# Leaving out the idle matrix products behind the spreading of the roots at three stage boundaries

## The reference

```python
for i in range(DEPTH):                                   # 2 layers
    h = _modulate(_rmsnorm(x, norm1_w[i]), sh1, sc1)     # the same for ctx
    y, yc = _retention(...) if i == 0 else _neighbourhood_attention(...)
    x = x + g1 * y
    h2 = _modulate(_rmsnorm(x, norm2_w[i]), sh2, sc2)
    x = x + g2 * _conv_ffn(h2, ...)
    if not last:                                         # layer 0 only
        ctx = ctx + cg1 * yc  # and its own norm and FFN
return _rmsnorm(x, final_norm_w)

def _rmsnorm(x, w):
    y = x * lax.rsqrt(jnp.mean(x * x, axis=-1, keepdims=True) + NORM_EPS)
    return y * w
```

## Time and profile before

| | |
|---|---|
| median of 3 runs | 1993.24 us (1992.49 to 1995.27) |
| the profiled execution: its own time | 1995.75 us |
| its span (first to last instruction) | 1993.8 us |
| TensorE busy | 1966.0 us, 99% of the span |
| VectorE busy | 1288.7 us, 65% |
| ScalarE busy | 718.4 us, 36% |
| idle products of `keep_busy` | 62, all by line 471 |
| mean granted TensorE clock | 0.996 of full |

### The profile page before, as it was taken

How to read it: one execution, slowest core, us unless ns; L and a number is a source line. 1 busy time by engine, 2 the same in 40 slices (tenths; PEclk the granted TensorE clock), 3 DMA queues, 4 the chain that set the end, 5 groups by cost and what they waited for, 6 DMA issues and landing times.

```text
span 1993.8 us, 29041 instructions
## 1 busy us (share of the span) xinstructions
PE 1966.0 (99%) x10628; PEld 1686.2 (85%) x10628; DVE 1288.7 (65%) x1976; ACT 718.4 (36%) x1111; POOL 93.2 (5%) x161
## 2 busy tenths in 40 slices
PE   9999999999999999999999999999999999999998
PEld 8888888888888888888888888888888778888886
DVE  7866645735645677765665467867777777467376
ACT  5433224223313343312331233365665543233243
POOL 0000000000000000000000000211111000000000
PEclk9999999999999999999999999999999999999999
DMA  7221321321221123233223323331111322223223
GB/s 310 99 85 64 106 64 54 106 73 55 85 95 64 54 64 95 95 124 115 94 94 122 116 95 127 123 99 52 53 48 48 106 85 95 95 95 103 86 95 106
DMA packets 51268, 186.56 MB, mean 94 GB/s; under 512 B 5680, under 2 KB 5680, under 8 KB 51184
## 3 DMA queue, kind: packets, MB, share of 16 engines
q1 hardware_dynamic: 37744, 136.73, 20.5%
q0 software_dynamic: 13440, 48.63, 7.5%
HBM read 181.15 MB, written 4.19 MB: 93 GB/s over the span
## 4 chain that ended last, share of the span: by engine, by line
PE 94%; DVE 2%; ACT 1%; DMA 1%; issue 1%; SPq 0%; DVEq 0%; ACTq 0%; POOLq 0%
PE acc L404 60%; PE acc L724 6%; PE o_ps L543 4%; PE acc L664 4%; PE o_ps L574 3%; PE acc L543 3%; PE o_ps L724 2%; PE acc L561 2%; PE acc L503 2%; PE acc L759 1%; PE o_ps L710 1%; PE o_ps L689 1%; PE acc L697 1%; DMA ada_start<-in_ada_first_dram 1%; PE o_ps L455 1%
## 5 line engine op out<-in xcount | busy, mean ns | idle before, releaser
L883 ACT ACTIVATE w_hi<-raw 128x1024 fp32r<-128x1024 f32 x223 | 236.0, 1058 | 582.1 <-PE acc L404 466.5
L404 PE MATMUL acc<-h_hi,w_hi 128*128 128x512 f32 x1520 | 434.3, 349 | 3.4 <-ACT u L1084 1.8
L1314 DVE TENSOR_TENSOR w_lo<-raw,w_hi 128x1024 fp32r<-128x1024 f32 x223 | 272.9, 1224 | 252.7 <-ACT w_hi L883 251.1
L404 PE MATMUL acc<-h_hi,w_lo 128*128 128x512 f32 x1520 | 434.9, 349 | 0.0
L404 PE MATMUL acc<-h_lo,w_hi 128*128 128x512 f32 x1520 | 433.5, 348 | 0.0
L404 PEld LDWEIGHTS acc<-h_hi,w_hi 128*128 128x128 f32 x1520 | 244.6, 188 | 44.0 <-ACT u L1084 2.5
L404 PEld LDWEIGHTS acc<-h_hi,w_lo 128*128 128x128 f32 x1520 | 244.1, 188 | 38.2
L404 PEld LDWEIGHTS acc<-h_lo,w_hi 128*128 128x128 f32 x1520 | 243.4, 188 | 38.5
L1486 DVE SCALAR_TENSOR_TENSOR x<-acc,mod,x 128x512 f32<-128x512 f32 (+3 forms) x137 | 82.0, 634 | 149.7 <-PE acc L404 120.8
L404 PE MATMUL acc<-act_hi,w_hi 128*128 128x512 f32 (+1 forms) x396 | 119.8, 356 | 1.3 <-DVE x L1486 1.3
L404 PE MATMUL acc<-act_hi,w_lo 128*128 128x512 f32 (+1 forms) x396 | 120.1, 357 | 0.0
(11 more groups left out here) (263 smaller groups left out, 3390.8 us busy)
## 6 DMA issues: line engine op xcount, KB each, us to landing
raw<-in_weights_dram SPq DMA_DIRECT2D x232, 512.0 KB, 3.4
ada_raw<-in_ada_dram POOLq DMA_DIRECT2D x80, 512.0 KB, 3.8
ada_start<-in_ada_first_dram SPq DMA_DIRECT2D x8, 1024.0 KB, 19.2
x<-in_x_in_dram SPq DMA_DIRECT2D x4, 768.0 KB, 7.1
park_dram<-x POOLq DMA_DIRECT2D x1, 2048.0 KB, 8.1
rel<-in_bias_dram POOLq DMA_DIRECT2D x16, 128.0 KB, 2.4
x<-park_dram POOLq DMA_DIRECT2D x2, 1024.0 KB, 6.8
out_dram<-x SPq DMA_DIRECT2D x8, 256.0 KB, 2.2
```

The source lines that it names most:

```text
L404: mm = nc.tensor.matmul(tile[:, c0:c0 + cn], wt[:, b * P:(b + 1) * P], mv[:, n, c0:c0 + cn], start=(n == 0 and m == 0), stop=(n == last an ...
L883: nc.scalar.activation(w_hi[i][:, :] if spare is None else spare[0], raw[r][:, :], ACT.Copy).then_inc(hi_split, 1)
L1314: nc.vector.tensor_tensor(lo, raw[r][:, :], hi.bitcast(F32), ALU.subtract).then_inc(lo_split, 1)
```

## The change

The idle products that stand between `spread_roots` and the next stage's first projection are left out at the three inner boundaries: 12, 12 and 8 of them. Those ahead of the spreading (4 within `final_sums`, 2 behind it) stay, as does everything on the other engines. No wait and no semaphore count changes, and the result is the same.

```diff
             final_sums(TOK)
             keep_busy(2)
             spread_roots(PARTS, True)
-            keep_busy(12)
+
             ffn(PARTS, spare1)
             final_sums(TOK)
             keep_busy(2)
             spread_roots(PARTS, True)
-            keep_busy(12)
+
             q = []
...
             final_sums(LAT)
             keep_busy(2)
             spread_roots(LATENT)
-            keep_busy(8)
+
             ffn(LATENT, spare3)
```

## The result

The changed kernel takes 1996.96 us in the median of 21 runs (1994.25 to 1998.17), the kernel before 1994.17 us in 21 runs interleaved with them (1992.49 to 1996.36). The ratio is 1.0013, 95% interval 1.0007 to 1.0019: slower by 0.13%, some 2.8 us. The 0.5 us flatters the forecast: the difference was forecast as +4.3 us and measured as +2.8, 1.5 less, and 0.9 of that is hidden because the kernel before came out at 1994.17 here and not at the 1993.24 that the forecast started from. That part is luck.

What follows compares the result with a forecast made beforehand. TensorE was taken to bound the kernel (94% of the chain). Removal gains 0; clock falls cost 1.3 + 1.5 + 1.5 = +4.3 us, added to the median 1993.24: 1997.5 us, range 1992.8 to 2000.4.

Steps and rivals of the forecast that it cites:

- The removed work was hidden: At the three inner boundaries, the 8.07 us of idle products lie beside the VectorE and ScalarE chain; removal takes nothing off.
- I take 0: Gain from an earlier first product at the three boundaries: 0 to 0.45 us possible in all, taken as 0.
- The pause brings the clock down: TensorE pauses of 3.30, 3.80 and 2.54 us at the boundaries are followed by its clock falling to 0.50.
- The likeliest case: A clock fall at each of the three boundaries, +4.3 us in all, own range +3.0 to +5.5; chance 0.46.
- The rival that nothing happens: At the boundaries the pauses are too short for the clock to fall, and 1993.2 us stays; chance 0.13.
- the spared third fall: The third boundary's 2.54 us pause brings no fall, the other two do: +2.8 us, 1996.0 us; chance 0.17.
- The pause at 7 us: From 7 to 9 us TensorE did nothing and the clock stayed 1.00, so about 2 us can be free.
- The rate: Under dense work, pairs start every 0.64 us at half clock, 0.35 at full: 0.45 us lost per us.
- The sum (+4.3): Net cost of falls at the three boundaries: 1.3, 1.5 and 1.5 us, together +4.3 us.
- the mean with a long fall: First boundary: mean of a short fall, 1.54 us, and a half-hidden long one, 2.3, less 0.6 of waiting.
- The fall at 1305 us: In the attention's first projections, half clock for 3.40 us in the profiled execution; may be absent in others.
- the pause at 1302 us: 1302.22 to 1304.75 us, 2.53 us with only transposes: one pause if transposes don't count, otherwise two under 1 us.

Runs made afterwards that it cites:

- double: 24, 24 and 16 idle products of 512 columns instead of 12, 12 and 8 in the kernel before; 1996.16 us against 1994.30, ratio 1.0009.
- plain: The kernel before with 48, 48 and 32 instructions of 128 columns in place of its idle products behind the spreadings; 1995.73 us against 1994.30, ratio 1.0005.
- fill: The kernel before plus 3 idle products each ahead of and behind the attention's first six transposes; 1993.56 us against 1994.30, ratio 0.9997.
- again: The changed kernel timed once more, without edits; 1996.81 us against 1993.46 for the kernel before, ratio 1.0016.
- b2: The kernel before without the 12 idle products of the second boundary only; 1993.62 us against 1993.85, ratio 1.0001.
- bare: The changed kernel also without the idle products ahead of the spreading, at all four boundaries; 1998.26 us against 1993.46 for the kernel before, ratio 1.0026.
- half: 6, 6 and 4 idle products instead of 12, 12 and 8 in the kernel before; 1995.45 us against 1993.46, ratio 1.0010.
- plain12: The kernel before with 24, 24 and 16 plain instructions of 128 columns in place of its idle products; 1993.70 us against 1993.85, ratio 1.0000.
- narrow: The kernel before with 24, 24 and 16 instructions of 64 columns in place of its idle products; 1994.49 us against 1993.85, ratio 1.0002.
- turned: The kernel before with 24, 24 and 16 transposes of 128 columns in place of its idle products; 1993.58 us against 1994.30, ratio 0.9999.

## Why the prediction was right, point by point

**The removed work was hidden.** Right: first products at 3.29 and 2.54 us behind the spreading as before, at the first and third boundary. `double` shows the other edge of the same fact.

**"I take 0"** for a gain. Wrong by 0.2 us at the second boundary. There the first product came 3.58 us behind the spreading instead of 3.80, and 3.57 to 3.66 in each run with none or only 6 of the 512-column products at that place and the ones ahead of the spreading kept (`plain` apart, whose filler outlasted the operand). Unlike elsewhere, VectorE reads the latent half of `x` and of the roots column by column there. Its four first multiplications (L1461), in the kernel before and in the changed one:

```profile
1274.38 3.00 DVE L1461 SCALAR_TENSOR_TENSOR scratch<-x,norm_a,o_ps 128x512 f32<-128x512 f32 x4 [1.25 <-PE o_ps L455]
```

```profile
1274.21 2.77 DVE L1461 SCALAR_TENSOR_TENSOR scratch<-x,norm_a,o_ps 128x512 f32<-128x512 f32 x4 [1.25 <-PE o_ps L455]
```

The same four took 2.99 us in `fill` and 2.93 in `double`, 2.77 to 2.78 in `again`, `b2` and `bare`, and 2.79 to 2.86 beside shorter or fewer products; at the first boundary they took 2.19 us with and without them. So the idle products slowed the chain that was to hide them, by 0.23 us; the prediction had dismissed this on the ground that VectorE begins first. What they compete for was not tried.

**The pause brings the clock down.** Right, and at all three boundaries, in two profiles. The likeliest case, a fall at each, was the one that came: short, long, short in the first profile, three short ones in the second. The rival that nothing happens is refuted by both, the spared third fall too, though `half` shows that a fall can be spared there. The median alone would have pointed to that rival: it was priced at +2.8 us, just what was measured, while the case that came had +3.0 to +5.5 as its own range. The third segment, 1.28 us longer in both profiles, decides between them.

The pause at 7 us, which the prediction took as the witness against a fall, was not a good one. TensorE stood still there for 2.25 us before 9.04. In `half`, `plain12` and `plain`, whose work up to that place is the same, it stood still for 2.73, 2.38 and 2.87 us, and a fall of 3.4 us began at 10.3, 10.0 and 11.2 us; in `fill`, with 2.35 us, none did. That the one profile of the kernel before showed no fall behind this pause didn't mean that such a pause is free.

**The price.** The rate was right: 0.64 against 0.35 us per pair. The sum (+4.3) was too high by 1.1 us against the segments of the same profile (+3.2) and by 1.5 against the median (+2.8); that the stated time was hit to 0.5 us all the same is the luck told above. Term by term, for the changed kernel: first boundary 1.3 predicted, 0.61 measured (0.82 in `again`). The fall ended at 713.76, so 2.95 us of it lay under work, worth 1.33; VectorE's pace gave back 0.72 of it, against 0.6 allowed. The larger part of the error is the mean with a long fall, which came in neither profile. Second: 1.5 predicted, 1.29 with the long fall and 0.29 with a short one. Of the long one 1283.76 - 1278.19 = 5.57 us lay under work, worth 2.5; less 1.29 and the 0.22 by which the work began earlier, 1.0 us was given back instead of 0.4. With the short fall of `again`, all of it under work and worth 1.54, it was 1.54 - 0.29 - 0.22 = 1.0 us as well. Third: 1.5 predicted, 1.28 in both profiles. There 1.54 - 1.28 = 0.26 us was given back, where the prediction took none. `double` bears these amounts out without any fall: where TensorE was late at full clock, 0.7, 1.1 and 0.4 us were given back at the three places. The mis-sized terms are the waits that swallow a fall (the products for the queries at the second boundary don't fill them as assumed) and the share of long falls at the first boundary.

**The fall at 1305 us** is one of chance, as suspected when the profiled execution was set against the median: absent in the first profile of the changed kernel, present in the second (1306 us) and in `narrow` (1304 us). So one execution can't price a change of this size: before alone ranges over 3.9 us in 21 runs.

**The transposes.** The prediction weighed a rule of the Trainium skill ("TensorE: Matmul & The Clock Gate", Part 4) by which transposes don't count for the clock. No run here bears it out: 24 of them held it as well as 24 plain instructions did (`turned`, `plain12`). Measurement decides; the pause at 1302 us was then two short pauses around work, and is more like `half`, where 1.89 us were enough.

**Open:** what decides whether a given pause is followed by a short fall, a long one or none. The runs show that it varies between executions of one kernel, and no experiment here controls it.

## What to carry to other kernels

Work that nobody reads can still earn its time: before taking it out, look at what the engine would do in its place, and at the granted clock behind comparable pauses in the same trace. Price such a fall by the rate at either level times the part of it that lies under work, and take off the waits of the consumers' own pace, which here gave back from 0.3 to 1 us of each fall. Filler has two edges: half of it protected only in some executions, and as soon as it outlasted the operand that was waited for, it delayed the next product by what it overran, of which the consumers' pace gave back from 0.4 to 1.1 us, less than half in two cases of three.

## What the runs showed of the hardware that I had not expected

- The clock can fall after the work has resumed: in `half` 1.4 us, in `b2` in the middle of the first chunk. The stall and its price stand at different places in the timeline.
- At the first boundary 24 instructions of 64 columns, over 2.79 us, were followed by a fall, and 24 transposes of 128 columns, over 2.78 us, were not. Each is one profile, and the mean clocks of the two kernels' executions (0.9975 and 0.9980) are too near to each other to tell whether the columns made the difference.
- A product of float32 operands runs as two instructions on TensorE: 24 products gave 48 instructions, and 12 of 512 columns took 10.5 us.
- VectorE's column-wise multiplication of `x` by the roots took 3.00 us for four beside 512-column products and 2.77 beside an idle TensorE.
